# Convolution ahead of the gate, the second block mean from a weighted sum, and moved output steps in a two-block transformer kernel

## The reference

```python
def layer_norm(x, g=None, b=None, eps=LN_EPS):
    mu = mean(x); var = mean(square(x - mu))
    y = (x - mu) * rsqrt(var + eps)
    return y * g + b                       # if g is given
def adaln(x, shift, scale):
    return layer_norm(x) * (1.0 + scale) + shift

def memory_cross_attention(h, mem_n, w_q, w_kv, w_o):      # in both layers: 4 heads of 256
    ...                                                    # softmax(q k) v
    return o @ w_o
def odd_mixer(h, w_qkv, rel_bias, w_o):                    # layer 1: 16 heads, bands of 9 chunks of 64
    ...
    return o @ w_o

# second part
h = adaln(x, shift1, scale1)
p = h @ w_in                                               # convolution input and recurrence input
u = causal depthwise conv of 31 taps (p_conv) + conv_b
y_conv = silu(layer_norm(u, conv_ln_g, conv_ln_b))         # 512 wide
...                                                        # recurrence over tokens gives y_rw
y_rw = layer_norm(y_rw, per head) * rw_lnx_g + rw_lnx_b
y_rw = (y_rw + bonus) * g                                  # 512 wide; g is the gate
y1 = concatenate([y_conv, y_rw]) @ w_out
x = layer_norm(ALPHA * x + gate1 * y1, ln1_g, ln1_b)       # the block norm
h2 = adaln(x, shift2, scale2)                              # the second norm, of the block norm's output
q = h2 @ peer_wq                                           # 16 columns of 128
...                                                        # top 16 of 128 keys, experts, last norm
```

## Time and profile before

| | us |
|---|---|
| median of three runs | 3362.38 |
| lowest and highest run | 3359.74, 3362.65 |
| profiled execution | 3356.46 |
| its span in the trace | 3355.1 |
| TensorE busy | 3204.5 (96%) |
| VectorE busy | 2220.2 (66%) |
| POOL busy | 1577.8 (47%) |
| ACT busy | 1357.5 (40%) |

### The profile page before, as it was taken

One profiled execution on the slowest core, in us unless ns is written; L12 is line 12 of the kernel. 1 busy time (PEld: TensorE's weight loads), 2 busy tenths in 40 slices (PEclk: granted clock), 3 DMA queues, 4 the chain that ended last, 5 costly groups with the idle time before them and its releaser, 6 DMA issues.

```text
span 3355.1 us, 48057 instructions
## 1 busy us (share of the span) xinstructions
PE 3204.5 (96%) x18545; PEld 2707.9 (81%) x18545; DVE 2220.2 (66%) x3856; ACT 1357.5 (40%) x2195; POOL 1577.8 (47%) x874
## 2 busy tenths in 40 slices
PE   8998999999999999999899998999999998999997
PEld 8886778888776778888677656899999997888886
DVE  5585656555445656552587663369998995888788
ACT  5554443322444543222453234333333773333332
POOL 1022234444332324444333022468887445888885
PEclk9998999999999999999999999999999999999999
DMA  8412114444221314443220022359897999999995
GB/s 261 149 62 76 63 63 138 138 151 138 95 82 51 101 51 138 140 136 101 72 76 8 27 76 76 123 205 317 314 326 280 308 305 329 371 351 357 356 350 212
DMA packets 304882, 584.76 MB, mean 174 GB/s; under 512 B 13520, under 2 KB 224464, under 8 KB 287376
## 3 DMA queue, kind: packets, MB, share of 16 engines
q1 hardware_dynamic: 252512, 373.32, 33.0%
q0 software_dynamic: 42496, 153.34, 12.8%
q10 hardware_dynamic: 9648, 55.02, 4.3%
HBM read 522.91 MB, written 58.72 MB: 173 GB/s over the span
## 4 chain that ended last, share of the span: by engine, by line
PE 66%; DVE 13%; POOL 9%; issue 7%; ACT 4%; DMA 1%; DVEq 0%; POOLq 0%; SPq 0%; ACTq 0%
PE bank L488 14%; PE bank L489 14%; PE bank L490 14%; POOL split_low L465 6%; PE twin L488 4%; PE twin L489 4%; PE twin L490 4%; PE bank L2953 3%; PE bank L2373 2%; PE bank L586 1%; POOL rows_arena L3319 1%; POOL rows_h L3319 1%; POOL rows_near L3319 1%; PE bank L2180 1%; PE twin L586 1%
## 5 line engine op out<-in xcount | busy, mean ns | idle before, releaser
L465 POOL TENSOR_TENSOR split_low<-weights,split_high 128x1024 fp32r<-128x1024 f32 x498 | 1217.7, 2451 | 1336.3 <-ACT split_high L457 1295.0
L488 PE MATMUL bank<-normed_high,split_high 128*128 128x384 f32 (+1 forms) x1968 | 726.0, 369 | 28.7 <-ACT normed_high L615 14.0
L489 PE MATMUL bank<-normed_low,split_high 128*128 128x384 f32 (+1 forms) x1968 | 714.7, 363 | 0.0
L490 PE MATMUL bank<-normed_high,split_low 128*128 128x384 f32 (+1 forms) x1968 | 714.7, 363 | 0.0
L457 ACT CAST split_high<-weights 128x1024 fp32r<-128x1024 f32 x554 | 570.8, 1046 | 332.2 <-PE bank L490 189.0
L488 PEld LDWEIGHTS bank<-normed_high,split_high 128*128 128x128 f32 x1968 | 372.6, 189 | 76.3 <-ACT normed_high L615 16.4
L489 PEld LDWEIGHTS bank<-normed_low,split_high 128*128 128x128 f32 x1968 | 372.8, 189 | 38.6 <-issue 2.4
L490 PEld LDWEIGHTS bank<-normed_high,split_low 128*128 128x128 f32 x1968 | 372.5, 189 | 38.6
L488 PE MATMUL bank<-split_high,wide_hidden_high 128*128 128x512 f32 x768 | 300.3, 391 | 11.3 <-DVE wide_hidden_low L3175 5.9
L489 PE MATMUL bank<-split_low,wide_hidden_high 128*128 128x512 f32 x768 | 299.5, 390 | 0.0
L490 PE MATMUL bank<-split_high,wide_hidden_low 128*128 128x512 f32 x768 | 299.3, 390 | 0.0
(11 more groups left out here) (648 smaller groups left out, 6254.7 us busy)
## 6 DMA issues: line engine op xcount, KB each, us to landing
weights<-in_w_ff SPq DMA_DIRECT2D x64, 1024.0 KB
weights<-in_peer_u SPq DMA_DIRECT2D x64, 1024.0 KB
weights<-in_peer_v SPq DMA_DIRECT2D x64, 1024.0 KB
weights<-in_cond_w SPq DMA_DIRECT2D x24, 1024.0 KB
early_table<-branch SPq DMA_DIRECT2D x128, 192.0 KB
gate_table<-arena SPq DMA_DIRECT2D x12, 2048.0 KB
lates<-early_table ACTq DMA_DIRECT2D x32, 768.0 KB
gates<-gate_table ACTq DMA_DIRECT2D x32, 768.0 KB
```

Source lines behind the costliest of these rows:

```text
L465: pool.do.tensor_tensor(lo, raw_unit(u), hi.bitcast(F32), ALU.subtract).then_inc(*pool.sig("split_low", u))
L488: pe.do.matmul(o, ah, bh, start=first, stop=False)
L489: pe.do.matmul(o, ah, bl, start=False, stop=False)
L490: return pe.do.matmul(o, al, bh, start=False, stop=last)
```

## The change

It edits four places. (1) In `mem_slots` query column 7 moves from slot 7 to 11, and the output steps are one each in slots 13, 15, 16, 17, 19 and 20; in `odd_slots` one slot holds only the splits and the output steps follow one slot later. (2) At the end of the recurrence, the taps and the convolution's means come ahead of the gate products on TensorE, and the convolution's squares and root ahead of the weight casts and of the high halves of operands 4 to 7 on ACT. (3) `dve_block_sum` also keeps a sum of gain times residual (`block_gain`), one sum of it over channels on TensorE and the sums of two constant columns (`pe_block_columns`) give the second mean, and the peer operands are made in the block end itself; `ada` is no longer called here, and the residual's own gain and bias come after the operands. ACT may split weights up to the third query unit during the out product. (4) All transposes of x stand behind query column 3.

```diff
-        def act_evacuate(stage, ids, dst, upto=None):
-            for c in range(2 * len(ids)):
+        def act_evacuate(stage, ids, dst, upto=None, cs=None):
+            for c in cs or range(2 * len(ids)):
                 act_split(min(2 * ids[0] + c + AHEAD, upto or 2 * len(chunks) - 1))
                 if c % 2:
...
-            pieces = {2: ("q", 5), 4: ("q", 6), 7: ("q", 7)}
-            pieces.update((m, ("o", n)) for m, n in ((11, 2), (15, 1), (16, 1), (19, 1), (20, 1)))
+            pieces = {2: ("q", 5), 4: ("q", 6), 11: ("q", 7)}
+            pieces.update((m, ("o", 1)) for m in (13, 15, 16, 17, 19, 20))
...
-                slots.append((("o",) if i < 6 or i == 9 else None, 24 + i))
+                slots.append((("o",) if 0 < i < 7 or i == 9 else None if i else ("split",), 24 + i))
...
+        def pe_block_columns():
+            bank, empty = banks.take("block_columns")
+            pe.wait_ge(empty)
+            for j, name in enumerate(("ln1_g_2", "ln1_b_2")):
+                for c in range(CT):
+                    last = pe.do.matmul(bank[:, j:j + 1], mean, col(name, c), start=c == 0, stop=c == CT - 1)
+            last.then_inc(*pe.sig("block_columns"))
...
         def pe_block_end(stage):
             norm, emptied = stage + "-", [("block_centered", stage, CT - 1)]
             pe_sum(norm, T, 0, 2, mean, dve_tmp.tile("block_total", stage), at("block_total", stage, CT - 2), emptied)
             pe_sum(norm, T, 1, 2, mean, x[:, CT - 1, :], at("block_sum", stage, CT - 1), emptied)
+            pe_sum(stage + "g", T, 0, 1, mean, dve_tmp.tile("block_gain", stage), at("block_gain", stage, CT - 1),
+                   [("block_level", stage)])
             for i in range(CT):
                 pe_square_sum(stage, i, CT, mean)
-
-        def act_block_end(stage, shift):
+            for i in range(CT):
+                pe_square_sum(PM, i, CT, mean)
...
+        def act_block_end(stage, shift, which):
             act_logs()
             for c in range(CT):
                 act_square(stage, c, x[:, c, :], T, at("block_centered", stage, c))
                 act_tmp.give(("square", stage, c), ("summed", stage, c))
             act_root(stage, CT - 1, LN_EPS, root)
             for c in range(CT):
+                s, empty = act_tmp.take("square", PM, c)
+                act.wait_ge(empty, at("peer_in", c), at("block_columns_kept", 1))
+                act.do.activation(s, y[:, c, :], ACT.Square, bias=block_shift[:, c:c + 1]
+                                  ).then_inc(*act.sig("square", PM, c))
+                act_tmp.give(("square", PM, c), ("summed", PM, c))
+            r, empty = act_tmp.take("peer_root")
+            act_root(PM, CT - 1, LN_EPS, r, T, empty)
+            act_tmp.give(("peer_root",), ("ada_scaled", PM, CT - 1))
+            act_split(2 * W["P", "q"][0] + AHEAD)
+            for c in range(CT):
+                act.wait_ge(at("ada_scaled", PM, c))
+                act.do.activation(y[:, c, :], y[:, c, :], ACT.Identity, scale=scale_1[:, 8 * which + c:8 * which + c + 1],
+                                  bias=mod[:, 24 * which + c:24 * which + c + 1]).then_inc(*act.sig("peer_out", c))
+                act.wait_ge(act.last)
+                act.do.copy(h_hi[:, c, :], y[:, c, :]).then_inc(*act.sig("operand_high", PM, c))
+            for c in range(CT):
                 act.wait_ge(at("block_scaled", stage, c))
...
+            gained = dve_tmp.tile("block_gain", stage)
+            dve.wait_ge(at("block_sum", stage, c), at("block_gain", stage, c - 1) if c else None)
+            if c == 0:
+                dve.do.tensor_scalar(gained, x[:, c, :], col(gain, c), None, ALU.mult
+                                     ).then_inc(*dve.sig("block_gain", stage, c))
+            else:
+                dve.do.scalar_tensor_tensor(out=gained, in0=x[:, c, :], scalar=col(gain, c), in1=gained, op0=ALU.mult,
+                                            op1=ALU.add).then_inc(*dve.sig("block_gain", stage, c))
...
+            level, empty = dve_tmp.take("block_level", stage)
+            dve.wait_ge(empty, at("summed", stage + "g", 0), at("block_columns_kept", 1))
+            dve.do.tensor_scalar(level, banks.tile("sum", stage + "-"), block_stat[:, 2:3], None, ALU.mult
+                                 ).then_inc(*dve.sig("dve_step"))
+            dve.wait_ge(dve.last)
+            dve.do.tensor_tensor(level, banks.tile("sum", stage + "g"), level, ALU.add
+                                 ).then_inc(*dve.sig("block_level", stage))
             for c in range(CT):
-                dve.wait_ge(at("root", stage), at("square", stage, c))
+                dve.wait_ge(at("block_level", stage), at("block_centered", stage, c))
+                dve.do.scalar_tensor_tensor(out=y[:, c, :], in0=x[:, c, :], scalar=col(gain, c), in1=level,
+                                            op0=ALU.mult, op1=ALU.subtract).then_inc(*dve.sig("block_shifted", stage, c))
+            dve_tmp.give(("block_level", stage), ("block_shifted", stage, CT - 1))
+            for c in range(CT):
+                dve.wait_ge(at("root", stage), at("block_shifted", stage, c))
+                dve.do.tensor_tensor(y[:, c, :], y[:, c, :], root, ALU.mult).then_inc(*dve.sig("peer_in", c))
+            for c in range(CT + 1):
+                if c < CT:
+                    dve.wait_ge(at("root", PM), at("peer_in", c), at("square", PM, c))
+                    dve.do.scalar_tensor_tensor(out=y[:, c, :], in0=y[:, c, :], scalar=block_shift[:, c:c + 1],
+                                                in1=act_tmp.tile("peer_root"), op0=ALU.add, op1=ALU.mult
+                                                ).then_inc(*dve.sig("ada_scaled", PM, c))
+                if c:
+                    dve.wait_ge(at("peer_out", c - 1), at("operand_high", PM, c - 1))
+                    dve.do.tensor_tensor(h_lo[:, c - 1, :], y[:, c - 1, :], h_hi[:, c - 1, :].bitcast(F32), ALU.subtract
+                                         ).then_inc(*dve.sig("operand_low", PM, c - 1))
+            for c in range(CT):
+                dve.wait_ge(at("square", stage, c))
                 dve.do.scalar_tensor_tensor(out=x[:, c, :], in0=x[:, c, :], scalar=col(gain, c), in1=root,
...
-            conv_some(taps, 12)
+            run(taps)
+            pe_block_columns()
+            pe_center("conv-", 4, conv_mean, lambda i: conv[:, i, :], lambda i: at("conv_kept", i) if i in CONV_PE else at("conv_tap", CONV_K - 1, i),
+                      [("conv_centered", 3)])
...
-            run(taps)
-            pe_center("conv-", 4, conv_mean, lambda i: conv[:, i, :], lambda i: at("conv_kept", i) if i in CONV_PE else at("conv_tap", CONV_K - 1, i),
-                      [("conv_centered", 3)])
             for i in range(4):
...
+            act_conv(CONV_PE[1])
             for c in range(4):
                 act_square(f"gn{c}", 0, a_hat[:, c, :], T, at("gn_centered", c))
                 act_tmp.give(("square", f"gn{c}", 0), ("summed", f"gn{c}", 0))
-            act_conv(CONV_PE[1])
             for c in range(4):
                 act_root(f"gn{c}", 0, GN_EPS, n_[c])
+            for i in range(4):
+                act_square("conv", i, conv[:, i, :], T, at("conv_centered", i))
+                act_tmp.give(("square", "conv", i), ("summed", "conv", i))
+            act_root("conv", 3, LN_EPS, root)
             act_split(2 * W["R", "o"][0] + AHEAD)
             for c in range(4):
                 act.wait_ge(at("rw_gated", c))
                 act.do.copy(h_hi[:, 4 + c, :], a_hat[:, c, :]).then_inc(*act.sig("mixed_high", RM, 4 + c))
-            for i in range(4):
-                act_square("conv", i, conv[:, i, :], T, at("conv_centered", i))
-                act_tmp.give(("square", "conv", i), ("summed", "conv", i))
-            act_root("conv", 3, LN_EPS, root)
...
-            act_evacuate((RM, "o"), W["R", "o"], lambda c: y[:, c, :], last_unit(("R", "o")))
-            act_block_end("block0", "ln1_b_2")
+            act_evacuate((RM, "o"), W["R", "o"], lambda c: y[:, c, :], 2 * W["P", "q"][0] + AHEAD - 1)
+            act_block_end("block0", "ln1_b_2", 1)
...
             run(taps)
+            dve_block_columns()
+            dve_conv_end(0)
...
-            dve_conv_end(0)
...
         def pe_peer():
-            pe_ada(PM, lambda c: at("block_out", "block0", c))
             ids = W["P", "q"]
-            pe_x_turned((0, 1))
             run(pe_first((PM, "q"), ids, h_tile, h_ready(PM), evacuated((PM, "q"))))
-            pe_x_turned((2, 3))
-            run(pe_product((PM, "q"), ids, h_tile, h_ready(PM), evacuated((PM, "q")), T, FIRST))
+            queries = pe_product((PM, "q"), ids, h_tile, h_ready(PM), evacuated((PM, "q")), T, FIRST)
+            next(queries)
+            pe_x_turned((0, 1, 2, 3))
+            run(queries)
...
         def act_peer():
-            act_split(2 * W["P", "q"][0] + AHEAD)
-            act_ada(PM, 1)
```

(4 more changed lines are left out.)

35 lines of the change are left out of this document (25 added, 10 removed).

## The result

The changed kernel takes 3380.03 us, the median of five runs (3376.89 to 3385.2), where the kernel before takes 3362.38 (five runs, 3359.74 to 3364.61): a ratio of 1.0052, with a 95% interval of 1.0041 to 1.0064, or 17.5 us more (13.8 to 21.5). I had forecast 3371.4 and a range that ends at 3379. The direction was right and the size half of what came.

What follows compares the result with a forecast made beforehand. TensorE, busy for 3204.5 of 3355.1 us, was taken as the bound, so only its short idle times counted. Nine terms summed to +9.0 us, which on the median of 3362.38 gave 3371.4, range 3359 to 3379.

Steps and rivals of the forecast that it cites:

- the convolution, +2.0: Convolution ahead of the gate: the 6.61 wait goes, but sums and late low halves delay the out product, +2.0 us.
- the term of the one-column sums: Ahead of the conv means: 16 one-column matmuls, two passes each, 32 x 0.09 = 2.9 us, delaying the means as much.
- Block sums, +4.3: Out product: eight more VectorE instructions and three POOL splits beside them make the last residual late, +4.3 us.
- Block end, -4.2: Last residual to first query matmul: 34.3 us becomes 30.1, as the second mean goes but shifted operands come, -4.2 us.
- first rows: Start of the query product: a wait of about 5.5 brings a few more slow rows, +0.5 us.
- transposes: Query product: all four transposes stand behind query column 3, where TensorE has no slack, +1.9 us.
- lower clock behind the wait: Query column 4: eight slow rows at 0.20 more behind the wait for the POOL's split, +1.7 us.
- the POOL's part: Ahead of query column 4: the POOL's split of unit 4 comes late, after its transpose wait and a DMA, +3.4 us.
- Attentions, -0.6: Moved slots: the two memory attentions cost +0.5 us together, the end of odd attention gains, -1.1 us.
- All later work shifts as a block: Behind the query product nothing is edited, so all later work was to move by the same amount.

Runs made afterwards that it cites:

- e3: The changed kernel with ACT's three casts of query units held back until the last residual is made; 3369.15 us, ratio 1.002 to the kernel before.
- e12: The changed kernel with the old slots of both the memory and odd attentions; 3373.02 us, ratio 1.0036 to the kernel before.
- e16: The changed kernel with the odd attention's slots taken back and the memory attentions' new; 3373.1 us, ratio 1.0042 to the kernel before.
- e4: The changed kernel with the POOL's split of query unit 4 ahead of its wait for the last transposed tile; 3372.7 us, ratio 1.0035 to the kernel before.
- e9: The changed kernel with one matmul of 16 columns in place of the 16 one-column matmuls, VectorE summing the results; 3374.76 us, ratio 1.0041 to the kernel before.
- e6: The kernel before with only the convolution moved ahead of the gate, no one-column sums, no new block norm; 3356.19 us, ratio 0.9986.

## Why the prediction was right or wrong

- **The direction and most mechanisms held.** Each of the five waits that I had forecast is there: 5.4 ahead of the out product (5.3 is what my times gave), 5.5 for the block sums, 4.5 ahead of the second squares, 5.8 ahead of the first query matmul (5.5), 3.3 ahead of column 4 (3.4).
- **The step that failed is the convolution, +2.0, measured +6.2 (4.5 in e3, e12 and e16).** The casts and the splits beside the low halves did what I had said: low halves 5.46 instead of 2.49. Mis-sized was the term of the one-column sums. I had 0.09 a row from four rows in 0.36 us, 2.9 in all. That average hides that the second row starts 0.03 behind the first and every later one 0.11 behind the one before: 32 rows take 3.49 at full clock (e3, e12, e16), and 3.94 in the changed kernel, whose last five fell to the lower clock. And I put the clock behind them at nothing. The 8 rows of the means took 6.61 instead of 3.60 in the changed kernel, 6.43 in e4 and 5.38 in e3, e12 and e16. These are all five traces that have the sums in that place, and in none of the other thirteen did the means take more than 3.68; e9, with one wide matmul in the same place, shows that it is the kind of the sums and not their place. With 1.0 and 3.0 added my 2.0 becomes 6.0 (measured 6.2), with 0.6 and 1.8 it becomes 4.4 (4.5). The rest of the term, -0.9 without the sums, is what e6 measured, -0.8. The Trainium skill, TensorE: Matmul & The Clock Gate, Part 1, puts the floor of such a row at 25 ns; here only the second of the 32 rows comes so soon, and the others are far above it.
- **Block sums, +4.3:** TensorE's wait grew by 4.4 (1.06 to 5.48). Right, with its cause (e3). The splits cost 5.7 where I had taken 5.3. 1.0 of lower clock behind the wait was not in the sum.
- **Block end, -4.2:** 34.3 to 30.1. Right to 0.1, but with luck twice. The pieces missed both ways: VectorE ends the shifted operands 14.0 behind the last residual where I had 12.9, and from the end of the squares to the first query matmul are 5.8 where I had 6.6. And the 34.3 of before holds 1.4 of lower clock in the second mean that five of seven traces don't have; against those the new block end saves 2.8.
- **Query product:** first rows +1.1 (0.5), transposes +2.0 (1.9), wait 3.34 (3.4), lower clock behind the wait 0 in the changed kernel and 1.6 in e12 (1.7). The last term is thus a thing of some executions, like the eight slow rows behind the wait of 2.14 from which I took it: five of seven traces with the old block norm have that wait without slow rows. The others are right, and e4 showed the POOL's part, which the diff doesn't.
- **Attentions, -0.6:** waits as worked out within 0.3 us, but the odd one gained 0.2 and not 1.1, and the clock may have taken more than that. Not measurable in the time.
- **"All later work shifts as a block"** is not quite so: behind 2107.6 the eleven kernels with the new block norm are 1.6 to 3.7 us longer than before, the six without it 0.3 to 1.6. TensorE's idle time there lies between 19.4 and 21.0 in all eighteen; much of the difference is clock. Why is open.
- **The sum.** From 1945 to 2107 the changed kernel is 13.2 us longer (e12: 13.1), where I had 9.6; that is the part that the experiments explain. The ratio says 17.5. Of the 4.3 between, 3.0 can be named: the trace of before, on which I built every term, has them as lower clock in the block end and the first query rows, and five of the seven traces with the old block norm do not, so against those the change costs 16.2 there. The stretch behind 2107.6 adds 1 to 3. How often each fall comes in the runs that were only timed is not known: e12 and e16, which differ from the changed kernel by slots alone, are 12.1 and 14.1 us over before by their ratios, each interval reaches 4 to 5 us to either side, and the recurrence alone can move a run by 8. My range left no room for the clock's own spread.

## What to carry to other kernels

A row of tiny matmuls on an otherwise full TensorE can cost more than its own time (here 3.9 us of them and 3.0 behind them): put them into one matmul with more columns and let VectorE add. Before a cast or a split is let run earlier, look which VectorE instructions with their operands in SBUF stand beside it, since one of them was stretched to about the split's length for each split that met such work. And when work is moved across a wait, look for other engines that wait for the same event: here the POOL waited for the transposes with a weight split queued behind. And before one trace is taken as the base of a sum, see in a second one which of its slow rows come again: 3.0 us of the stretches forecast here did not.

## What the runs showed of the hardware

Behind 32 rows of one column (3.94 us) most of TensorE's next 8 rows of 512 columns were 0.85 apart where 0.43 is usual for them, although TensorE had not been idle; behind two rows of 16 columns (0.29 us) they were not. The granted clock had already fallen within the one-column rows (0.56 over their last microsecond). The one-column rows themselves were 0.11 apart at full clock and 0.21 at the lower one. And the same code in the recurrence ran at a granted clock of 0.66 over 20 us of one execution and 1.00 in others, with a difference of 5 to 8 us in its length.
